# Reordering three joints of a block kernel: the end of the gated recurrence, the first expert tiles behind the scores, the first value tile

## What is computed

```python
def rglru_mixer(h, in_w, conv_w, conv_b, ra_w, ra_b, ri_w, ri_b, lam, out_w):
    xb, gb = jnp.split(h @ in_w, 2, axis=-1)              # 2 x 1408 channels
    xb = causal_depthwise_conv(xb, conv_w, conv_b)
    r, i = sigmoid(blocks(xb) @ ra_w + ra_b), sigmoid(blocks(xb) @ ri_w + ri_b)
    log_a = -LRU_C * softplus(-lam) * r
    a, u = exp(log_a), sqrt(-expm1(2 * log_a)) * (i * xb)
    hs = associative_scan(a, u)                            # over the 256 tokens
    return (hs * gelu(gb)) @ out_w                         # 1408 -> 1024

def peer_ffn(h, q_w, subkey1, subkey2, expert_u, expert_v):
    q = h @ q_w                                            # 8 heads x 2 x 128
    s1, s2 = q[..., 0, :] @ subkey1, q[..., 1, :] @ subkey2
    # top 16 of 128 in each, top 16 of their 256 sums, softmax g over those
    act = gelu(expert_u[expert] . h)
    return sum(g * act * expert_v[expert])
```

## Time and profile before

| what | value |
|---|---|
| time, median of 3 runs | 2524.07 us (2521.89 to 2526.58) |
| the profiled execution: its own time | 2525.84 us |
| its span | 2524.1 us |
| mean granted clock of TensorE | 0.982 |
| TensorE busy | 2453.1 us, 97% of the span |
| VectorE, ScalarE, GpSimd busy | 1831.7, 1246.8, 1230.0 us |

### The profile page before, as it was taken

The page is one execution under the profiler, slowest core; times in us unless marked ns, Lnnn a source line. Parts: engine busy times, 40 slices in busy tenths (PEclk is TensorE's granted clock), DMA queues, the critical chain, the costliest instruction groups (busy, mean ns, idle before and its releaser), DMA issues.

```text
span 2524.1 us, 47109 instructions
## 1 busy us (share of the span) xinstructions
PE 2453.1 (97%) x18074; PEld 2275.1 (90%) x18074; DVE 1831.7 (73%) x3366; ACT 1246.8 (49%) x2150; POOL 1230.0 (49%) x525
## 2 busy tenths in 40 slices
PE   7999999989899999999999999999999999999999
PEld 7999999988899999998888888889999999888887
DVE  6857783668749899987777775563997999555555
ACT  6345543455555544444444454555454444444444
POOL 5547787645679977760000014456997676100000
PEclk9999999989999999999999998999999999999999
DMA  5435787732456655548777763334665454566664
GB/s 172 137 93 184 239 318 254 266 117 83 135 176 193 201 159 155 156 143 280 253 252 258 257 193 100 101 109 151 198 194 174 155 158 153 184 192 192 192 192 142
DMA packets 126063, 457.94 MB, mean 181 GB/s; under 512 B 13984, under 2 KB 15392, under 8 KB 125600
## 3 DMA queue, kind: packets, MB, share of 16 engines
q1 hardware_dynamic: 118512, 425.56, 53.4%
q10 hardware_dynamic: 7344, 29.49, 3.3%
HBM read 453.95 MB, written 1.05 MB: 180 GB/s over the span
## 4 chain that ended last, share of the span: by engine, by line
PE 84%; DVE 9%; issue 3%; ACT 2%; DMA 1%; POOL 1%; SPq 0%; DVEq 0%; POOLq 0%; ACTq 0%
PE mm L1297 28%; PE ms L1337 28%; PE mm L812 17%; PE ms L1318 3%; DVE work L1994 1%; POOL low L1937 1%; DVE hs L1994 1%; PE ms L819 1%; DVE work L1988 1%; PE ms L827 1%; DVE scratch L1994 1%; DVE work L1991 1%; PE mm L981 1%; PE mm L819 1%; DVE mm L1988 0%
## 5 line engine op out<-in xcount | busy, mean ns | idle before, releaser
L1937 POOL TENSOR_TENSOR low<-ring,high 128x1024 fp32r<-128x1024 f32 (+2 forms) x502 | 1216.2, 2437 | 915.3 <-ACT high L1548 758.7
L1802 ACT ACTIVATE high<-ring 128x1024 fp32r<-128x1024 f32 x506 | 535.8, 1059 | 355.6 <-PE ms L1337 324.6
L1297 PE MATMUL mm<-hs,high 128*128 128x256 f32 x4096 | 520.4, 280 | 3.4 <-ACT high L1548 3.4
L1337 PE MATMUL ms<-high,wts 128*128 128x512 f32 x2048 | 510.8, 392 | 0.0
L2573 DVE TENSOR_TENSOR low<-ring,high 128x1024 fp32r<-128x1024 f32 x256 | 313.4, 1225 | 248.3 <-ACT high L1802 248.3
L1297 PEld LDWEIGHTS mm<-hs,high 128*128 128x128 f32 x4096 | 486.8, 188 | 3.8 <-issue 3.8
L1337 PEld LDWEIGHTS ms<-high,wts 128*128 128x128 f32 x2048 | 384.2, 188 | 84.0
L1548 ACT ACTIVATE high<-ring 128x1024 fp32r<-128x1024 f32 (+2 forms) x252 | 258.2, 1030 | 126.5 <-PE mm L812 98.1
L812 PE MATMUL mm<-hs,high 128*128 128x256 f32 x2192 | 286.3, 284 | 7.5 <-DVE parts L1988 3.9
L812 PEld LDWEIGHTS mm<-hs,high 128*128 128x128 f32 x2192 | 268.2, 191 | 12.9 <-ACT high L1548 7.2
L1337 PE MATMUL ms<-low,wts 128*128 128x512 f32 x1024 | 276.1, 391 | 3.0 <-DVE low L2573 3.0
(11 more groups left out here) (342 smaller groups left out, 3070.0 us busy)
## 6 DMA issues: line engine op xcount, KB each, us to landing
ring<-w_peer_experts SPq DMA_DIRECT2D x512, 512.0 KB, 3.9
work<-w_mod ACTq DMA_DIRECT2D x48, 512.0 KB, 5.6
ring<-w_late_mods SPq DMA_DIRECT2D x48, 512.0 KB, 4.5
ring<-w_ffn_up SPq DMA_DIRECT2D x44, 512.0 KB, 5.1
ring<-w_peer_q SPq DMA_DIRECT2D x32, 512.0 KB, 3.7
ring<-w_fox_in SPq DMA_DIRECT2D x32, 512.0 KB, 3.5
ring<-w_lru_in SPq DMA_DIRECT2D x22, 512.0 KB, 3.5
ring<-w_gates SPq DMA_DIRECT2D x16, 512.0 KB, 3.6
```

The source lines that it names most:

```text
L1297: ins_ = pe.matmul(mm[:, s_ % BANKS, 0:T], w_[:, k * P:(k + 1) * P], hs[:, b_, k, :], start=pass_ == 0 and k == 0, stop=pass_ == 2 and k = ...
L1337: ins_ = pe.matmul(ms[:, 2 * c + half, :], wts[:, s_ % 3, b_, c * P:(c + 1) * P], v_[:, half * 512:(half + 1) * 512], start=s_ == 0 and pa ...
L1802: act.activation(high[:, (q0 + i) % CUT, :], ring[:, n_ % RAW, :], ACT.Copy) \
L1937: pool.tensor_tensor(low[0:rows, cut_slot, 0:width], ring[0:rows, raw_slot, 0:width], high[0:rows, cut_slot, 0:width].bitcast(F32), ALU.su ...
```

## The change

- **Banks and order of the recurrence's output.** It rotates over three banks, so three outputs are open: (0,0) (1,0) (2,0) (0,1) (1,1) (2,1), then by pairs. All later banks of layer 0 shift up to the end of its scores (queries start on bank 3 instead of 1; the last scores lie in banks 3, 0, 1, 2 instead of 1, 2, 3, 0); layer 1 keeps its banks.
- **ACT.** Tile 0 of `lru_out` is cut within the loop, in the round of group 10, ahead of the evacuation of its g product. Behind the gates of 9 and 10: round products 5 and 6, cut tile 1, round 7, the last roots, cut tile 2, round 8 to 10.
- **POOL.** The low parts of products 5 to 7 follow the cut of tile 1, those of 8 to 10 the cut of tile 2.
- **DVE.** The t + 1 of the coefficients is a step of its own. Behind the loop: scans 6 and 7, t + 1 of 9 and 10, coefficients of 9 and 10, scans 8 to 10. The reciprocal of the final norm moves into the round of group 3.
- **PEER.** Up to query tile 3, `ahead` cuts one tile further. One U tile is cut ahead of score evacuation 0 and one ahead of evacuation 4.
- **Values.** The low part of V tile 0 is made ahead of `weigh_hidden` of 127 instead of behind the last `weights_low`.

```diff
-LRU_OUT = [(0, 0), (1, 0), (0, 1), (1, 1)] + [(m, half) for m in range(2, KD) for half in range(2)]
+LRU_BANKS = 3
+LRU_OUT = [(m, half) for half in range(2) for m in range(LRU_BANKS)] + [(m, half) for m in range(LRU_BANKS, KD) for half in range(2)]
...
-        _last = (_last + 1) % (3 if _kind == "ple_gate" else 2 if _kind in TWO_BANKS else BANKS)
+        _last = (_last + 1) % (LRU_BANKS if _kind in ("ple_gate", "lru_out") else 2 if _kind in TWO_BANKS else BANKS)
...
                 ahead("lru_in", 2 * j + 1)
+                if j == RT - 1:
+                    ahead("lru_out", 0, 0)
...
             lru_act(RT - 2)
             lru_act(RT - 1)
+            lru_high(5)
+            lru_high(6)
             ahead("lru_out", 0, 1)
-            for k in range(5, 9):
+            lru_high(7)
+            lru_roots(RT - 1)
+            ahead("lru_out", 0)
+            for k in range(8, RT):
                 lru_high(k)
-            lru_roots(RT - 1)
-            for k in range(9, RT):
-                lru_high(k)
-            ahead("lru_out", 0)
...
                 for j in range(16):
-                    ahead(f"peer{L}_q", j)
+                    ahead(f"peer{L}_q", j, CUT if j < BRIDGE[i] else CUT - 1)
...
                 for c in range(TT):
+                    ahead(f"peer{L}_experts", c, 0)
                     for g in range(4):
                         evacuate(OUT0[f"peer{L}_scores"] + 4 * c + g, es[:, c, 4 * g:4 * g + 4, :], width=512)
...
-                        if name == "lru_out" and i == 1:
-                            for k in range(5, RT):
+                        if name == "lru_out" and i in (1, 2):
+                            for k in (range(5, 8), range(8, RT))[i - 1]:
                                 lru_low(k)
...
+            def lru_denominator(j):
+
+                dve.wait_ge(sem("lru_tanh"), j + 1)
+                ts(lr[:, j, :], lt[:, j, :], 1.0, None, ALU.add, None, "lru_t_read")
+
             def lru_coefficients(j):
 
-
-                dve.wait_ge(sem("lru_tanh"), j + 1)
                 r_, i_ = lru_gate(0, j), li[:, j, :]
-                ts(lr[:, j, :], lt[:, j, :], 1.0, None, ALU.add, None, "lru_t_read")
...
                 if j >= 2:
+                    lru_denominator(j - 2)
                     lru_coefficients(j - 2)
+                if j == 3:
+                    dve.wait_ge(sem("final_root"), 1)
+                    S.did(dve.reciprocal(final_rstd, final_rstd))
                 if j >= 5:
                     lru_scan(j - 5)
+            lru_scan(6)
+            lru_scan(7)
+            lru_denominator(RT - 2)
+            lru_denominator(RT - 1)
             lru_coefficients(RT - 2)
-            for k in range(6, 9):
+            lru_coefficients(RT - 1)
+            for k in range(8, RT):
                 lru_scan(k)
-            lru_coefficients(RT - 1)
-            lru_scan(9)
-            lru_scan(10)
             dve.wait_ge(sem("mod1_summed"), 1)
             finish_mods(24, 48, mm[:, 3, 0:24], "mod1_taken")
             finish_gains(1)
-            dve.wait_ge(sem("final_root"), 1)
-            S.did(dve.reciprocal(final_rstd, final_rstd))
...
                     else:
+                        if k == KEYS - 1:
+                            values_low(0)
                         if groups_before(k):
                             weigh_hidden(k)
                         if k >= KEYS - 3:
                             weights_low(k - KEYS + 3)
                 for s_ in range(KEYS):
-                    values_low(s_)
+                    if s_:
+                        values_low(s_)
```

## The result

| | before | changed |
|---|---|---|
| median of 6 runs each | 2526.97 us (2521.89 to 2530.28) | 2511.36 us (2507.15 to 2516.47) |
| ratio, 95% interval | | 0.9941 (0.9925 to 0.9956) |
| the profiled execution | 2525.84 us | 2511.46 us |

The changed kernel is faster: by the ratio 0.59%, or 14.9 us (11.1 to 18.9) of 2526.97; the two medians are 15.6 us apart. I had forecast 18.1 us, 0.72%: inside that interval, but at its far end. The two profiled executions are 14.4 us apart. Both kernels scatter by 8 to 9 us from run to run, more than any one joint is worth, so the joints are read from the profiles, start to start, and whole runs only for the sign.

The account below looks back on a forecast made before the run. TensorE carries 84% of the span, so time is won only where PE stands still or its clock is halved. 5.8 + 4.8 + 3.9 + 3.6 = 18.1 us takes 2524.07 to 2506.0; range 2503 to 2509.5, with rivals 2501.0 to 2511.5.

Parts of the forecast that it names:

- 2.4 for each layer: Queries: cutting tiles 4 and 5 earlier wins 2.4 us per layer of the 2.63 lost from tile 4 to 6.
- The lower bound: Queries: only 0.5 us gained per layer if POOL, four lows in a row, or h's low parts take over.
- the paragraph on the port: Recurrence's end: GpSimd locks out two-input VectorE instructions; scan 8 would end 2 us later, with the same sum.
- Recurrence, "5.8 us": Recurrence's end: PE restarts near 631.4 instead of 634.59, (3,0) at 647.4 instead of 653.23; bounds 2.5 to 7.5 us.
- about 1.3: Recurrence's output: new stall of about 1.3 us before (2,1), tile 5 being cut behind ACT's square and rounding of output 0.
- Reciprocal, "nothing": Recurrence loop: moving the 1.75 us reciprocal into round 3, where DVE waits 1.44 us, costs nothing there.
- U tiles, 2.3 and 1.6: First U tiles: two cuts moved ahead among score evacuations win 2.3 us in layer 0, 1.6 in layer 1.
- V tile, 1.78 for each layer: First V tile: low part made in DVE's idle time before weigh_hidden of 127 wins 1.78 us per layer (4.53 - 2.75).
- Rival 1: Recurrence's end gives back its gain through DVE and POOL blocking and half clock: 2.5 instead of 5.8 us, 2509.3; chance 0.17.
- Rival 2: Queries and scores: PE waits for POOL or the last evacuation instead of ACT; 2 us left of 8.7, 2512.7; chance 0.06.
- Rival 3: Whole change doesn't do what it says: only the V tiles count, 3.6 us, 2520.5, within 0.2%; chance 0.03.
- Rival 4: Recurrence's output: clock stays at 0.50 from restart to norm, 35 us more, 2541, slower than before; chance 0.02.

Follow-up runs that it names:

- e1: Changed kernel with the cut ahead in the query stage undone, tiles 4 and 5 cut as before; ratio to before 0.9943, median 2515.35 us.
- e2: Changed kernel, but POOL holds query tile 5's low part until VectorE has made all eight low parts of h; ratio to before 0.9921, median 2509.20 us.
- e3: Changed kernel with the whole recurrence part undone (banks, output order, order of work, reciprocal), the rest kept; one run, 2519.87 us.
- e4: Changed kernel with the new order of work, but the recurrence's output by pairs in two banks as before; one run, 2513.4 us.
- e5: Changed kernel with three open outputs and banks kept, but the old order of work at the recurrence's end; one run, 2515.2 us.
- e8: Changed kernel with the reciprocal of the final norm back at the end of the recurrence; one run, 2515.06 us.
- e6: Changed kernel with the three U tiles cut behind the last score evacuation as before, banks as changed; one run, 2514.20 us.
- e9: e2 with layer 1's queries started on bank 3, moving its last score off U tile 0's bank; ratio to before 0.9919, median 2506.21 us.
- e7: Changed kernel with V tile 0's low part made behind the last of the weights' low parts as before; one run, 2519.19 us.
- e11: The changed kernel again without an edit, on the same chip as e9 and e10; ratio to before 0.9928, median 2508.16 us of six runs.
- e10: e9 with recurrence output by pairs in two banks and layer 0's queries set to start on bank 3; ratio to before 0.9934, median 2510.46 us.

## Why the prediction was right or wrong

**The step that failed is the queries' "2.4 for each layer".** It measured 0.25 and 0.18 between the two profiles. So 4.4 of the 4.8 us of this term are missing, which is more than the whole gap between forecast and joints (18.1 - 14.5 = 3.6 us). I followed the cut through ACT, the cut slots and the raw slots, and asked whether POOL would have the low parts in time. I didn't ask what POOL's low part does to the engine beside it. The lower bound had the words "POOL, four lows in a row, or h's low parts take over", and the second half of them came true, below even its 0.5. Yet I had the rule and the row in hand: the paragraph on the port used them for one scan of the recurrence and went no further, though h's low parts also read two inputs from SBUF and have PE waiting for the last of them. The prediction counted every place where the moved cut must wait, and not every place that waits longer because of it. e1 and e2 show it from both sides: 8.10 without the cut ahead, 7.8 with it, 6.25 with it and POOL held back.

**Recurrence, "5.8 us": right in its mechanism, 6.38.** The size has some luck in it: against e3, without the second slow stretch of before, it is 5.35. Step by step from the start of the sums: restart 10.58 forecast (631.4 - 620.82), 10.03 measured; (0,0) 5.29 and 5.29; (1,0) and (2,0) 6.02 and 5.71; stall before (2,1) "about 1.3", 1.00; the half behind it 1.06 and 1.55; (3,0) at 26.6, measured 26.03. That it is the order of work, as the working had it, e4 and e5 show. What the working didn't weigh is that the third bank brings the stall and nothing else at this joint; I took the banks and the order as one part. The rule of the port held where I had applied it, only on the instructions behind the scan: two products of DVE beside tile 2's low part took 2.97 us against 0.98 for the next two, the 2 us I had named, with PE not yet waiting. VectorE and GpSimd in the changed kernel:

```profile
630.44 2.97 DVE L1993 TENSOR_TENSOR work<-work 128x256 f32<-128x256 f32 x2
...
634.68 0.98 DVE L1993 TENSOR_TENSOR work<-work 128x256 f32<-128x256 f32 x2
```

```profile
629.76 2.80 POOL L1942 TENSOR_TENSOR low<-ring,high 128x1024 fp32r<-128x1024 f32 x1 [0.73 <-ACT high L1549]
```

**Reciprocal, "nothing": right** (e8).

**U tiles, 2.3 and 1.6: right**, 2.57 and 1.61. Both causes hold: the cuts (e6) and the bank (U0 against U1 in the changed kernel, e4, e9). Layer 0 gained 0.27 more than I took: U tile 0 started 9.11 us behind the scores' start before and 7.14 now, 1.97 us less, where the idle time in brackets had said 1.72.

**V tile, 1.78 for each layer: right**, 1.78 and 1.76 (e7).

**The rivals.** Rival 1 (the recurrence gives back) fell: no stretch at half clock but the first. Rival 2 (hidden anyway) was half true, in the queries and not behind the scores; its 2 us left of 8.7 were in fact 0.43 + 4.18 = 4.6. Its reason, that PE would wait for POOL, was not it. Rival 3 fell. Rival 4, the half clock through the output stage, and with it the cycling of PSUM banks that the Trainium skill (TensorE: Matmul & The Clock Gate, "A second HAM failure mode: psum-queue depth-cycling") warns of, fell too: three banks in turn ran at 0.98 and 1.00.

**The number.** The changed kernel's 2511.36 lies 1.9 us outside the forecast's own range (2503 to 2509.5) and just inside the one with the rivals (to 2511.5). 2506.0 was worked out from the three runs shown then, median 2524.07; six runs gave 2526.97, 2.9 us of the 5.4 between forecast and measurement. By the joints 3.6 us are missing, the 4.4 of the queries less 0.8 that the other terms gave beyond their forecast; the scatter of whole runs covers the rest. By the ratio, 0.9928 forecast, 0.9941 measured.

## What to carry to other kernels

When a step is moved to an earlier place, go through what runs beside it there on every engine, not only through what it waits for: a GpSimd instruction put beside VectorE instructions with two SBUF inputs held them up for nearly its own length (2.1 us for 2.5), and TensorE, which reads their result, paid. One wait on a semaphore, with which the moved step starts behind them, brought 1.8 us of the 2.4 forecast for each layer. And look at parts of a change that came as one, such as an order of work and a number of banks, one at a time: here the first was worth 6.7 to 7.8 us and the second cost 1.4 at its own joint.

## What the hardware showed that I had not expected

**The same short stall, with and without a fall of the clock.** Behind the 1.1 us stall inside query tile 4 the clock was granted in full in 11 of 16 places and halved for some 3.4 us in 5, for 1.6 us more. All five lie in kernels with an edit (e3 twice, e5, e6, e7); the four places of the changed kernel, its profile and e11, have none. That the stall is the cause isn't shown either: before and e1 stand still for 1.22 us one tile later, waiting for ACT's cut, and in their four places the clock stayed at 1.00. Why in one layer and not in the other stays open.

**Two rates at one granted clock.** Tiles of 24 products take 2.72 us (16 of them 1.98) or 2.83 us (16 of them 2.05) with the granted clock at 1.00 in both. Layer 1's queries in the changed kernel, and the windows of e10 over its queries and first U tiles of layer 0:

```profile
1717.29 2.05 PE L813 MATMUL mm<-hs,high 128*128 128x256 f32 x16
```

```profile
680.00:712.00 32.00, 31.65 (x266) 1.00 0.63 192
722.00:800.00 78.00, 78.00 (x665) 1.00 0.65 200
```

The slower rate begins at a restart of PE or in the middle of a stage, and holds: for all of the queries of layer 1 here and in e4, e7, e9 and e11 (29.11 us from tile 6 to the scores instead of 28.04: the 1.07 us above), for the queries and 52 U tiles of layer 0 in e9 and e10 (1.1 and 5.6 us), and for 31 and 50 U tiles of layer 1 in e7 and e8 (3.4 and 5.3 us). In the profile of before it isn't in these stretches, though it is in the first block, and in the recurrence's loop of both kernels it comes and goes from group to group. Its cause I didn't find; no experiment was aimed at it. It is likely a part of why whole runs scatter by some 8 us, and a reason to judge an edit of 1 or 2 us by its joint.
